# The end of a decoder layer: weight row on GpSimd, mean square taken earlier, left halves stored from ScalarE's queue

## What is computed

```
h = h + (silu(n2 @ w_ffn_gate) * (n2 @ w_ffn_up)) @ w_ffn_down
return h * rsqrt(mean(h * h, axis=-1) + EPS) * lnf_g
```

## Time and profile before

| | us |
|---|---|
| median of 3 runs | 950.41 |
| lowest and highest of them | 950.18, 951.73 |
| the profiled execution's own time | 951.74 |
| the profiled span | 949.9 |
| TensorE's last product ends | 942.74 |
| last store issued | 947.30 |

### The profile page before, as it was taken

One profiled execution on the slowest core, in us unless ns is written; L12 is line 12 of the kernel. 1 busy time (PEld: TensorE's weight loads), 2 busy tenths in 40 slices (PEclk: granted clock), 3 DMA queues, 4 the chain that ended last, 5 costly groups with the idle time before them and its releaser, 6 DMA issues.

```text
span 949.9 us, 10934 instructions
## 1 busy us (share of the span) xinstructions
PE 905.5 (95%) x3953; PEld 736.1 (77%) x3953; DVE 622.6 (66%) x801; ACT 399.7 (42%) x653; POOL 338.6 (36%) x242
## 2 busy tenths in 40 slices
PE   3989999999998889999999999999999999999996
PEld 2766777877777668888888888888888888888885
DVE  5657896435348996556646566566565995687666
ACT  6349733433247632333232323333324444445465
POOL 2033334344556465454554554555552000000000
PEclk9999999999999999999999999999999999999999
DMA  8010110203100222323223223332245963333334
GB/s 284 27 45 22 45 45 23 79 11 111 45 1 22 67 71 96 122 89 122 97 82 133 89 100 122 89 122 89 83 160 190 405 218 99 100 97 94 99 89 177
DMA packets 93789, 96.42 MB, mean 102 GB/s; under 512 B 5628, under 2 KB 63528, under 8 KB 93736
## 3 DMA queue, kind: packets, MB, share of 16 engines
q1 hardware_dynamic: 83368, 76.84, 23.8%
q10 hardware_dynamic: 10368, 18.88, 6.6%
HBM read 71.33 MB, written 24.38 MB: 101 GB/s over the span
## 4 chain that ended last, share of the span: by engine, by line
PE 86%; DVE 6%; ACT 3%; issue 2%; POOL 2%; DMA 1%; SPq 0%; DVEq 0%; ACTq 0%; POOLq 0%
PE bank L1586 21%; PE bank L1588 21%; PE bank L1587 21%; PE bank L1474 7%; PE bank L1476 7%; PE bank L1475 7%; DVE T_lo L1237 1%; PE bank L1517 1%; POOL w_lo L587 1%; PE bank L1491 1%; PE bank L1528 1%; DMA h<-in_x 1%; DVE xc L1094 1%; ACT nT_hi L621 1%; DVE nT_lo L1209 1%
## 5 line engine op out<-in xcount | busy, mean ns | idle before, releaser
L582 POOL TENSOR_TENSOR r_lo<-gu_raw,r_hi 128x512 fp32r<-128x512 f32 x87 | 121.4, 1396 | 75.0 <-ACT r_hi L800 74.9
L582 POOL TENSOR_TENSOR r_lo<-wsum_S,r_hi 128x512 fp32r<-128x512 f32 x63 | 95.3, 1512 | 123.3 <-ACT r_hi L800 123.3
L1586 PE MATMUL bank<-T_hi,r_lo 128*128 128x512 f32 x336 | 131.0, 390 | 3.7 <-DVE u L1329 1.7
L1587 PE MATMUL bank<-T_lo,r_hi 128*128 128x512 f32 x336 | 130.7, 389 | 0.0
L1588 PE MATMUL bank<-T_hi,r_hi 128*128 128x512 f32 x336 | 130.7, 389 | 0.0
L1586 PE MATMUL bank<-d_hi,h_lo 128*128 128x512 f32 x308 | 119.8, 389 | 0.0
L1587 PE MATMUL bank<-d_lo,h_hi 128*128 128x512 f32 x308 | 119.8, 389 | 0.0
L1588 PE MATMUL bank<-d_hi,h_hi 128*128 128x512 f32 x308 | 119.8, 389 | 0.0
L1586 PE MATMUL bank<-nT_hi,r_lo 128*128 128x512 f32 x280 | 109.4, 391 | 2.7 <-DVE nT_lo L1209 2.1
L800 ACT CAST r_hi<-gu_raw 128x512 fp32r<-128x512 f32 x87 | 54.2, 623 | 133.1 <-PE bank L1588 133.1
L1588 PE MATMUL bank<-nT_hi,r_hi 128*128 128x512 f32 x280 | 109.0, 389 | 0.0
(11 more groups left out here) (192 smaller groups left out, 1690.2 us busy)
## 6 DMA issues: line engine op xcount, KB each, us to landing
h_raw<-hid_ops ACTq DMA_DIRECT2D x72, 256.0 KB, 2.6
gu_raw<-in_w_ffn_gate SPq DMA_DIRECT2D x22, 512.0 KB, 3.6
gu_raw<-in_w_ffn_up SPq DMA_DIRECT2D x22, 512.0 KB, 4.7
hid_ops<-hid SPq DMA_DIRECT2D x44, 256.0 KB, 2.2
dn<-in_w_ffn_down SPq DMA_DIRECT2D x44, 256.0 KB, 10.9
hid_ops<-hsum_S SPq DMA_DIRECT2D x33, 256.0 KB, 2.6
w_raw<-in_w_in SPq DMA_DIRECT2D x12, 512.0 KB, 3.6
h<-in_x SPq DMA_DIRECT2D x8, 512.0 KB, 7.4
```

The source lines that it names most:

```text
L582: pool.tensor_tensor(lo_of(n)[:], a_block(f, name), f32(hi_of(n)[:]), ALU.subtract)\
L1586: pe.matmul(bank, s_lo, m_hi, start=(opens and j == 0), stop=False, skip_group_check=True)
L1587: pe.matmul(bank, s_hi, m_lo, start=False, stop=False, skip_group_check=True)
```

## The change

Three things are done to the end of the kernel.

1. The right halves of the last four tiles are multiplied by the weight row on GpSimd, as soon as ScalarE has read them for the sum of squares (`sq_ok`). VectorE's L1426, a product of the half with a factor and a row, becomes a product with the factor alone (a `tensor_scalar`), which waits for GpSimd through a new semaphore, `fin_gain_ok`.
2. `last_scale` is divided into `last_root` (the four small instructions) and `last_scale` (the product), and VectorE's order changes: the variance of a tile comes ahead of the scaling of the tile in front. ScalarE's order changes with it, `last_sqrt` going ahead of `scale_out`.
3. The stores of the four left halves leave SyncE's queue and are issued from ScalarE's (`store_left`), each after its own `scale_out` has ended. The right halves remain on SyncE's queue.

```diff
@@ SyncE
                 else:
-                    sp_q.wait_ge(fin_act_ok, j + 1)
-                    sp_q.dma_start(outf[cols(t), 0:512], h[:, t, 0:512]).then_inc(stored, 16)
                     sp_q.wait_ge(fin_ok, j - 3)
                     sp_q.dma_start(outf[cols(t), 512:1024], h[:, t, 512:1024]).then_inc(stored, 16)
@@ GpSimd
             for n in range(5, NE):
                 split_entry(n)
+
+            for m in range(4):
+                pool.wait_ge(grow_in, 48)
+                pool.wait_ge(sq_ok, 2 * TT + 5 + m)
+                pool.tensor_tensor(quad(m, 0, 1), quad(m, 0, 1), g_row[:, 512:1024], ALU.mult).then_inc(fin_gain_ok, 1)
@@ ScalarE
+            def store_left(j):
+                t = FIN_ORDER[j]
+                act.wait_ge(fin_act_ok, j + 1)
+                act.dma_start(outf[cols(t), 0:512], h[:, t, 0:512]).then_inc(stored, 16)
+
...
             scale_out(3)
             scale_out(4)
             last_sqrt(1)
+            store_left(4)
             last_squares(2)
+            last_sqrt(2)
             scale_out(5)
-            last_sqrt(2)
+            store_left(5)
             last_squares(3)
+            last_sqrt(3)
             scale_out(6)
-            last_sqrt(3)
+            store_left(6)
             scale_out(7)
+            store_left(7)
@@ VectorE
+            def last_root(m):
+                n = 2 * TT + 4 + m
+                norm_rsqrt(NB + 2 + TT + 2 + m, n, n + 1, fin_rstd_ok)
+
             def last_scale(m):
                 n = 2 * TT + 4 + m
-                norm_rsqrt(NB + 2 + TT + 2 + m, n, n + 1, fin_rstd_ok)
-                dve.scalar_tensor_tensor(out=quad(m, 0, 1), in0=quad(m, 0, 1), scalar=rstd[:, n:n + 1],
-                                         in1=g_row[:, 512:1024], op0=ALU.mult, op1=ALU.mult).then_inc(fin_ok, 1)
+                dve.wait_ge(fin_gain_ok, m + 1)
+                dve.tensor_scalar(quad(m, 0, 1), quad(m, 0, 1), rstd[:, n:n + 1], None, ALU.mult).then_inc(fin_ok, 1)
@@
             add_down("M3", 0)
             last_variance(0)
             add_down("M3", 1)
-            last_scale(0)
+            last_root(0)
             last_variance(1)
             add_down("M3", 2)
+            last_root(1)
+            last_variance(2)
+            last_scale(0)
+            add_down("M3", 3)
+            last_root(2)
+            last_variance(3)
             last_scale(1)
-            last_variance(2)
-            add_down("M3", 3)
             last_scale(2)
-            last_variance(3)
+            last_root(3)
             last_scale(3)
```

More of the change, by code:

```diff
@@ L244, in hymba_pool_rglru_block @@
         fin_ok = sem("fin_ok")
+        fin_gain_ok = sem("fin_gain_ok")
         vT_ok = sem("vT_ok")
```

## The result

| | before | after |
|---|---|---|
| median, 22 runs each | 951.23 | 952.98 |
| lowest and highest | 950.12, 952.35 | 951.63, 953.69 |
| profiled execution, its span | 951.74, 949.9 | 953.32, 951.5 |
| TensorE's last product ends | 942.74 | 942.87 |
| from there to the end of the span, "the tail" | 7.16 | 8.63 |

A forecast was written before the change was run, and what follows sets the result against it. TensorE, busy 95% of the span, bounds the kernel; the change acts only behind its last product. Last scaling +1.51, second queue -0.38, in all +1.1 on the median of 950.41: 951.5 us, range 949.8 to 952.5.

The forecast's parts named there:

- GpSimd holds VectorE's fast scaling: VectorE's scalings of the last tiles: each stands until GpSimd's product ends, finishing 0.28 us after it; 0.48 alone.
- A store on ScalarE holds its engine for 0.38: Left-half stores on ScalarE's queue: each issue priced at SyncE's spacing, 0.38 us; squares of tile 2 begin 0.33 later.
- rival of the free issue: Left-half stores on ScalarE: issuing costs next to nothing, the squares' delay shrinks by 0.3, total 951.2 us; chance 0.12.
- The variance is not held: VectorE's variance beside GpSimd stays short; the rival that it stands gave +1.9, 952.3 us, chance 0.09.
- VectorE doesn't get in first: Tile 2's shared signal: GpSimd starts before tile 0's scaling; the rival, VectorE first, gave +0.5, 950.9 us, chance 0.09.
- The last scaling starts 1.51 later: End of the kernel: root of the last tile at 946.85, last scaling of both engines at 947.68 instead of 946.17.
- step 6: Last stores: left half issued last, at 948.43 instead of 947.30, +1.13; the second queue gives back 0.38 us.
- step 7: Last issue to end of span: the same 2.6 us, span 951.0, tail off by some 0.2 either way.
- +1.1: Whole kernel: the predicted slowdown in us, +1.51 for the last scaling less 0.38 for the second queue.
- The "no hold-up" rival: GpSimd doesn't hold VectorE up: last add stays at 942.76, left store at 946.90, -0.4, 950.0 us; chance 0.12.

## Why the prediction was right and where it was wrong

- **GpSimd holds VectorE's fast scaling.** Right, with its size: 0.28 from GpSimd's end to the end of a scaling, 0.28 measured; 0.48 alone, 0.47 to 0.49 measured; GpSimd's product 1.29, and 1.26 to 1.30 measured. Measured in that very pair, and shown by removal (8.63 to 7.35).
- **A store on ScalarE holds its engine for 0.38.** Right in kind, and a little short. The squares of tile 2 start at 941.33 with 0.42 of idle time ahead of them, where the forecast had 0.33, so the rival of the free issue is out. The 50 ns that the Trainium skill gives (DMA: Bandwidth & Descriptors, Anatomy of one DMA) are for an issue by GpSimd, which no run here makes; they are not the price on ScalarE, whose issue at 940.86 took 0.37.
- **The variance is not held, VectorE doesn't get in first.** Right: both variances take 0.21 beside GpSimd, and GpSimd was there before the scaling each time, by 0.12.
- **The last scaling starts 1.51 later.** 1.64 (5.07 behind TensorE against 3.43). Of the 0.13 the longer hold of the store on ScalarE makes 0.10: the squares of tile 2 start 1.54 ahead of TensorE's end instead of 1.64. GpSimd's products start 0.14 to 0.15 behind the read instead of 0.10, twice on the path. All but 0.03 of that comes back, since they take 1.28 and 1.26 instead of 1.29 and the squares of tile 3 follow the add 0.02 sooner. The two scalings beside GpSimd's last product end 0.68 after it, as forecast.
- **Steps 6 and 7, "0.38 is what the second queue gave back" and "the same 2.6 to the end".** This is the step of the mechanism that failed. The last issue did move by the sum of step 6 (5.82 behind TensorE against 4.56: +1.26, which is 1.64 - 0.38), but the time from issue to end, which step 7 held fixed, grew from 2.60 to 2.81: a store that sets out with another lands later, since the two share DMA engines that are full (0.97 of the 1.4 us of a pair). Here step 7's "0.2 either way" covered the size, though it was put down to the queue; without the hold-up it is 3.15. The stores alone, in the old order, cost 0.20 rather than give 0.38. The rows had it: the pair took 2.58 from the first issue to the landing of the second, which is 2.0 for one half and some 0.6 for another 256 KB, and no earlier issue of the second half changes that.
- **The sum against the median.** This is the largest miss, and without it the measured time would lie inside the range, which would end at 953.3 instead of 952.5. The forecast put its +1.1 on 950.41, the median of three runs; the 22 runs of before have a median of 951.23, 0.8 more. The tail grew by 1.47, forecast was 1.13: on 950.41 that makes 951.9. Against 950.41 + 1.13 the measured median is 1.44 higher: 0.82 for the base, 0.34 for the tail (0.13 from the last scaling and 0.21 from the stores), and 0.28 by which the medians differ more than the tails do, which is inside the interval of 0.9 to 2.1. The range took in the unknown costs of the end and not the spread of a kernel whose clock rises at different times; three runs between 950.18 and 951.73 had shown it. Against the kernel before in the same measurement, the forecast's ratio of 1.0011 is inside the interval, in its lower part.
- **What the text didn't price.** That the new order costs 0.53 even without GpSimd was in the sum (two scalings ahead of the root) but was never set apart from the hold-up. The "no hold-up" rival had the last issue right (4.16 behind TensorE, measured 4.20 with GpSimd's product left out), and was too good by its stores: 7.35 against 7.16 is the number that it should have had.

## What to carry to other kernels

Before work goes to GpSimd to relieve VectorE, look for the moments at which both would be released by the same signal: VectorE's fast one-tensor form (1.44 for 0.48 here) and products of two tensors in SBUF (1.80) stand until GpSimd's product has ended, and what queues behind them stands too. A slower form of the same instruction that isn't held can be the faster one (tail 7.88 against 8.63), and if that form is as slow as the instruction it replaced, GpSimd's help is worth nothing. And at the end of a kernel count the bytes from the first issue of the last stores: in these traces a second queue issued them sooner but didn't move them sooner. Where a kernel's runs differ by more than the effect, read the effect in a stretch of the trace that starts at a common event.

## What the runs showed of the hardware

- A `tensor_scalar` of 128x512 in float32 takes 0.48 us alone and 1.44 to 1.57 beside a GpSimd product; it waits for a GpSimd memset as well (1.11). With the sum as a second output it takes 0.74 beside the product and 0.75 alone.
- A product of two 128x1 columns on VectorE took 0.55 instead of 0.22 beside GpSimd's product.
- GpSimd's first instruction after 211 us of rest took 1.30, the three behind it 1.26 to 1.30 (the row at 936.52, under the results).
- Two 256 KB stores issued together on two queues land after 2.6 to 2.7 us, one alone after 2.0; the 16 DMA engines are full for 1.4 us (0.97, 375 GB/s) and for 0.7 us (0.96, 372 GB/s).
- A store issued by ScalarE puts its next instruction off by some 0.42 us, with 0.34 to 0.38 for the issue itself.
- Behind the same idle time of TensorE of some 2.1 us its clock fell to the lower level in four of 14 executions.
